# Scaling x by a product with diagonals in the prologue of a hybrid layer, and pairing the two products of a block inverse

## The reference

```python
def _rms(x, gain):
    y = xf * lax.rsqrt(jnp.mean(xf * xf, axis=-1, keepdims=True) + EPS)
    return (y * gain).astype(x.dtype)

mod = c @ p['w_ada'] + p['b_ada']
shift, scale, gate = jnp.split(mod, 3, axis=-1)
h = _rms(x, p['norm_gain']) * (1 + scale[:, None, :]) + shift[:, None, :]
... = _split_in(h @ p['w_in'])          # 9,296 columns

# in _gated_delta, per chunk of 64 tokens and head
L = jnp.where(tri_strict, jnp.einsum('bnhid,bnhjd->bnhij', kb, kc) * decay, 0.0)
tinv = lax.linalg.triangular_solve(eye + L, eye, left_side=True, lower=True)
```

## Time and profile before

| | |
|---|---|
| median of three runs | 1803.33 us (1802.0 to 1804.93) |
| the profiled execution | 1802.76 us, of which the span is 1800.9 us |
| TensorE, weight loads | 1724.2 us busy (96%), 1610.2 us (89%) |
| VectorE, ScalarE, GpSimd | 911.9 us (51%), 635.0 us (35%), 242.1 us (13%) |
| granted clock of TensorE | 0.990 of full speed on average |
| DMA queues | 286.15 MB moved, 159 GB/s over the span |

### The profile page before, as it was taken

How to read it: one execution, slowest core, us unless ns; L and a number is a source line. 1 busy time by engine, 2 the same in 40 slices (tenths; PEclk the granted TensorE clock), 3 DMA queues, 4 the chain that set the end, 5 groups by cost and what they waited for, 6 DMA issues and landing times.

```text
span 1800.9 us, 28716 instructions
## 1 busy us (share of the span) xinstructions
PE 1724.2 (96%) x11182; PEld 1610.2 (89%) x11182; DVE 911.9 (51%) x1694; ACT 635.0 (35%) x1169; POOL 242.1 (13%) x353
## 2 busy tenths in 40 slices
PE   4999999999999899999999999989999998999998
PEld 2999999999999899999999988877887897999986
DVE  4544555754564776896222244344444446563433
ACT  5523524543443532233333242334333445020200
POOL 0111111212121710421311200000000121000000
PEclk9999999999999999999999999999999998999999
DMA  9222334677876843446654230124215797652342
GB/s 339 81 84 82 105 107 149 202 238 223 271 227 193 262 158 117 145 139 203 204 179 158 96 130 24 36 84 128 60 47 199 273 356 252 210 189 72 118 140 76
DMA packets 235760, 286.15 MB, mean 159 GB/s; under 512 B 43185, under 2 KB 193230, under 8 KB 235500
## 3 DMA queue, kind: packets, MB, share of 16 engines
q1 hardware_dynamic: 227916, 280.57, 48.7%
q10 hardware_dynamic: 7552, 3.73, 0.7%
q0 software_dynamic: 160, 0.05, 0.0%
HBM read 179.39 MB, written 104.92 MB: 158 GB/s over the span
## 4 chain that ended last, share of the span: by engine, by line
PE 67%; issue 14%; DVE 5%; POOLq 4%; ACT 2%; POOL 1%; DMA 1%; DVEq 1%; SPq 1%; ACTq 0%
PE PS L2203 29%; PE PS L1056 10%; PE PS L418 7%; PE PS L1162 5%; PE PS L664 3%; PE PS L637 3%; PE PS L650 2%; POOLq L1795 1%; DVE R L2338 1%; POOLq L1793 1%; PE PS L639 1%; PE PS L638 1%; DVE hf L2350 1%; PE PS L2237 1%; POOL R L1859 1%
## 5 line engine op out<-in xcount | busy, mean ns | idle before, releaser
L2203 PE MATMUL PS<-HH,WL 128*128 128x352 f32 (+1 forms) x1728 | 385.3, 331 | 0.0
L2203 PE MATMUL PS<-HH,WH 128*128 128x352 f32 (+1 forms) x1728 | 373.3, 324 | 0.0
L2203 PE MATMUL PS<-HL,WH 128*128 128x352 f32 (+1 forms) x1728 | 372.3, 323 | 0.0
L2203 PEld LDWEIGHTS PS<-HH,WH 128*128 128x128 f32 (+1 forms) x1728 | 296.2, 188 | 0.3
L2203 PEld LDWEIGHTS PS<-HL,WH 128*128 128x128 f32 (+1 forms) x1728 | 293.5, 188 | 0.2
L2203 PEld LDWEIGHTS PS<-HH,WL 128*128 128x128 f32 (+1 forms) x1728 | 288.4, 189 | 2.9
L2325 DVE TENSOR_TENSOR WL<-Wraw,WH 128x2048 fp32r<-128x2048 f32 (+1 forms) x37 | 87.9, 2377 | 90.4 <-ACT WH L1917 89.2
L2338 DVE SCALAR_TENSOR_TENSOR R<-R,colA 128x1059 f32<-128x1059 f32 x72 | 97.2, 1349 | 5.5
L1937 ACT ACTIVATE R<-PS 128x1056 f32<-128x1056 f32 (+1 forms) x49 | 51.5, 1051 | 134.1 <-PE PS L2203 133.8
L689 ACT ACTIVATE pr<-PS,amx 128x128 f32<-128x128 f32 (+8 forms) x66 | 48.5, 734 | 127.5 <-DVE amx L730 127.5
L1056 PE MATMUL PS<-FH,VL 128*128 128x352 f32 x384 | 86.3, 333 | 4.6 <-DVE FL L980 3.4
(11 more groups left out here) (349 smaller groups left out, 2842.5 us busy)
## 6 DMA issues: line engine op xcount, KB each, us to landing
scratch_proj<-R SPq DMA_DIRECT2D x72, 576.0 KB, 3.3
Wraw<-in_w_in SPq DMA_DIRECT2D x36, 1024.0 KB, 6.9
job<-scratch_proj SPq DMA_DIRECT2D x18, 512.0 KB, 6.2
fr<-scratch_u SPq DMA_DIRECT2D x16, 528.0 KB, 5.7
gr<-scratch_proj SPq DMA_DIRECT2D x16, 528.0 KB, 3.9
job<-scratch_proj SPq DMA_DIRECT2D x9, 768.0 KB, 7.5
Wraw<-in_w_ada SPq DMA_DIRECT2D x6, 1024.0 KB, 9.5
R<-scratch_gcum SPq DMA_DIRECT2D x9, 512.0 KB, 6.3
```

Of the source, the lines that this page charges most:

```text
L2203: last = pe.matmul(PS[0:m, 3 * (p % 2) + b, 0:TB], w[:, u % 2, k, j * P:j * P + m], x[:, k, b * TB:(b + 1) * TB], start=(k == 0 and first) ...
```

## The change

In the prologue the squares of tiles 3, 8 and 7 (`X_ON_DVE`: third, fourth and eighth place of the order, counted from 0) move from ScalarE to VectorE, as one `tensor_tensor_reduce` each. VectorE no longer scales `R`; it makes a 128x128 diagonal matrix of each tile's scales in the space of `dcy`. The groups of k = 0 and 1 (`RAW` = 256 features) are made by TensorE as a full product of unscaled x with this diagonal, and the other 768 features of each tile are scaled in place by GpSimd. The first modulation columns are handled between the two sets of scales. The order of x groups, modulations and first chunk steps on TensorE is written anew, with the places where ScalarE (`n` = 6, 11, 16) and VectorE (6, 12, 18) take part in the modulation and where ScalarE splits the first weights (now n = 6).

In the side work f3 is no longer a step of its own: step f2 of tile t makes its eight products alternately with the eight f3 products of tile t - 1, and a last f2 step stands after the eighth tile. The matrices of the two lie in opposite corners: SBUF partitions 0 to 63 to PSUM partitions 64 to 127, and 64 to 127 to 0 to 63.

Semaphores that are only renamed are left out of the diff.

```diff
@@ -284,6 +284,10 @@
         return max(n for n, (kk, g) in enumerate(XG) if kk == k) + 1
 
     X_ORDER = [0, 1, 2, 3, NT, 4, 5, 6, 7]
+    X_HALVES = ((0, 5), (5, 9))
+    X_ON_DVE = (3, 4, 8)
+    RAW = 256
+    diag = dcy[:, :, :, :].rearrange("p a b c -> p (a b c)").rearrange("p (t n) -> p t n", n=P)
 
 
     def col_of(c):
@@ -1459,8 +1463,9 @@
     W_INV, N_INV = S0 // 2 + 20, 17
     F0 = 120
     for t in range(NT):
-        for i in range(3):
-            side[at(F0 + 3 * t + i)] = (f"f{i + 1}", t)
+        side[at(F0 + 3 * t)] = ("f1", t)
+        side[at(F0 + 3 * t + 1)] = ("f2", t)
+    side[at(F0 + 3 * NT - 1)] = ("f2", NT)
     L0, L_STEP, Q0, Q_STEP = 4 * 31, 6, 4 * 48, 10
     for t in range(NKT):
         if t <= NT:
@@ -1631,7 +1636,7 @@
             sp.dma_start(N21[t % 2], tile3(scr["nl"][t, 0:HB])[:, :, HB:P]).then_inc(s_fl[t % 2], 16)
 
         def inverse_out(t):
-            sp.wait_ge(s_sr, turns["f3", t] + 1)
+            sp.wait_ge(s_sr, turns["f2", t + 1] + 1)
             sp.dma_start(scr["xt"][t], XTs[t % 2].rearrange("p h n -> p (h n)")).then_inc(s_fs[t % 2], 16)
 
         def latent_in(t):
@@ -1753,10 +1758,10 @@
                     v_out(t)
                     if t + 2 <= NT:
                         v_in(t + 2)
-                if kind == "f3":
-                    inverse_out(t)
-                    if t + 2 < NT:
-                        inverse_in(t + 2)
+                if kind == "f2" and t:
+                    inverse_out(t - 1)
+                    if t + 1 < NT:
+                        inverse_in(t + 1)
                 if slot == at(S0 + 4 * NT + 6):
                     for t in range(2):
                         v_in(t)
@@ -1808,6 +1813,10 @@
         pool.dma_start(rows[72:96, 1], a["b_ada"][0].rearrange("(c p) -> c p", p=P)).then_inc(s_vecs, 16)
         for i, name in enumerate(("dn_out_norm", "q_nope_norm", "k_nope_norm")):
             pool.dma_start(rows[96 + i:97 + i, 1], a[name]).then_inc(s_vecs, 16)
+        for c, t in enumerate(X_ORDER):
+            n = rows_of(t)
+            pool.wait_ge(s_xn, c + 1)
+            pool.tensor_scalar(R[0:n, t, RAW:D], R[0:n, t, RAW:D], xst[0:n, 1, c:c + 1], None, ALU.mult).then_inc(s_pad, 1)
         pool.wait_ge(s_colc, 2)
         pool.wait_ge(s_hl, NG)
         pool.memset(stage[:, 0, TOK:TPAD], 0.0)
@@ -1900,13 +1909,14 @@
             act.activation(modr[:, i % 2], PS[0:98, 3 + i % 2, 0:P], ACT.Copy).then_inc(s_modr, 1)
         act.wait_ge(s_xst, 1)
         for n, t in enumerate(X_ORDER):
+            if n in X_ON_DVE:
+                continue
             if n == 2:
                 rows_of_modulation(0)
                 act.wait_ge(s_cols, 2)
                 act.activation(colB[:, :], PS[:, 0, 0:99], ACT.Copy).then_inc(s_colc, 1)
-            rows_t = P if t < 8 else DEC
             act.wait_ge(s_x[t // 4], 16)
-            act.activation(hf[0:rows_t, 0:2].rearrange("p a b -> p (a b)"), R[0:rows_t, t], ACT.Square, accum_out=xst[0:rows_t, 0, n:n + 1]).then_inc(s_xss, 1)
+            act.activation(hf[:, 0:2].rearrange("p a b -> p (a b)"), R[:, t], ACT.Square, accum_out=xst[:, 0, n:n + 1]).then_inc(s_xss, 1)
             act.drain()
 
         def split_hi(u):
@@ -1964,10 +1974,10 @@
         for n in range(NG):
             g, k, w = x_group(n)
             cols = slice(512 * g, 512 * g + w)
-            if n == 2:
+            if n == 6:
                 split_hi(0)
-            if n in (2, 9, 15):
-                rows_of_modulation(1 + (2, 9, 15).index(n))
+            if n in (6, 11, 16):
+                rows_of_modulation(1 + (6, 11, 16).index(n))
             act.wait_ge(s_mod, k // 2 + 1)
             act.wait_ge(s_xT, n + 1)
             if n >= NHF:
@@ -2075,10 +2085,12 @@
                 act.wait_ge(s_nas[1], 16 * (NT + 1))
             act.activation(A1, PS[0:HB, 6].rearrange("p (h n) -> p h n", h=H), ACT.Copy).then_inc(s_sr, 1)
         if kind == "f2":
-            act.activation(Pm, PS[HB:P, 7].rearrange("p (h n) -> p h n", h=H), ACT.Copy).then_inc(s_sr, 1)
-        if kind == "f3":
-            act.wait_ge(s_xi, 2)
-            act.activation(XTs[t % 2][0:HB, :, HB:P], PS[0:HB, 6].rearrange("p (h n) -> p h n", h=H), ACT.Copy).then_inc(s_sr, 1)
+            if t < NT:
+                x = act.activation(Pm, PS[HB:P, 7].rearrange("p (h n) -> p h n", h=H), ACT.Copy)
+            if t:
+                act.wait_ge(s_xi, 2)
+                x = act.activation(XTs[(t - 1) % 2][0:HB, :, HB:P], PS[0:HB, 6].rearrange("p (h n) -> p h n", h=H), ACT.Copy)
+            x.then_inc(s_sr, 1)
 
     def act_decay(act, step):
         if step == 0:
@@ -2133,12 +2145,16 @@
 
         def x_back(n):
             g, k, w = x_group(n)
-            pe.wait_ge(s_xn, (4, 9, 5)[g])
+            pe.wait_ge(s_xn if k < RAW // P else s_pad, (4, 9, 5)[g])
             if n >= 2:
                 pe.wait_ge(s_hf, n - 1 if n < 16 else max(n - 3, 15))
             for t in range(4 if g < 2 else 1):
                 r = P if g < 2 else DEC
-                last = pe.transpose(PS[:, x_bank(n), t * P:t * P + r], R[0:r, 4 * g + t, k * P:(k + 1) * P], ident[0:r, 0:r])
+                out, rows_t = PS[:, x_bank(n), t * P:t * P + r], R[0:r, 4 * g + t, k * P:(k + 1) * P]
+                if k < RAW // P:
+                    last = pe.matmul(out, rows_t, diag[0:r, X_ORDER.index(4 * g + t), 0:r], start=True, stop=True)
+                else:
+                    last = pe.transpose(out, rows_t, ident[0:r, 0:r])
             last.then_inc(s_xT, 1)
 
         def first_chunk(k):
@@ -2159,32 +2175,33 @@
         pe.transpose(PS[:, 0, 0:99], rows[0:99, 1], ident[0:99, 0:99]).then_inc(s_cols, 1)
         modulation_columns(0)
         pe.wait_ge(s_colc, 2)
-        for n in range(2):
+        for n in range(4):
             x_back(n)
         for half in range(2):
+            x_back(4 + half)
             modulation(1, half)
-        for n in range(2, 4):
-            x_back(n)
+        x_back(6)
         modulation_columns(1)
-        for n in range(4, 6):
-            x_back(n)
-        for half in range(2):
-            modulation(2, half)
-            x_back(6 + half)
+        x_back(7)
         for k in range(2):
             first_chunk(k)
             x_back(8 + k)
+        modulation(2, 0)
+        x_back(10)
+        modulation(2, 1)
         modulation_columns(2)
-        x_back(10)
+        x_back(11)
+        first_chunk(2)
+        x_back(12)
+        first_chunk(3)
+        x_back(13)
         for half in range(2):
             modulation(3, half)
-            x_back(11 + half)
-        for n in range(13, 16):
-            x_back(n)
+            x_back(14 + half)
         modulation_columns(3)
         for n in range(16, 18):
             x_back(n)
-        for k, tiles in zip(range(2, KD), ((18, 19), (20, 21), (22,), (23,), (), ())):
+        for k, tiles in zip(range(4, KD), ((18, 19), (20, 21), (22, 23), ())):
             first_chunk(k)
             for n in tiles:
                 x_back(n)
@@ -2274,10 +2291,10 @@
                 x = pe.transpose(PS[0:HB, 6, h * HB:(h + 1) * HB], XTs[t % 2][0:HB, h, 0:HB], ident[0:HB, 0:HB])
         if kind == "f2":
             for h in range(H):
-                x = pe.matmul(PS[HB:P, 7, h * HB:(h + 1) * HB], N21[t % 2][:, h], A1[:, h], start=True, stop=True)
-        if kind == "f3":
-            for h in range(H):
-                x = pe.matmul(PS[0:HB, 6, h * HB:(h + 1) * HB], Pm[:, h], XTs[t % 2][HB:P, h, HB:P], start=True, stop=True)
+                if t < NT:
+                    x = pe.matmul(PS[HB:P, 7, h * HB:(h + 1) * HB], N21[t % 2][:, h], A1[:, h], start=True, stop=True)
+                if t:
+                    x = pe.matmul(PS[0:HB, 6, h * HB:(h + 1) * HB], Pm[:, h], XTs[(t - 1) % 2][HB:P, h, HB:P], start=True, stop=True)
         x.then_inc(s_sd, 1)
 
     @block.tensor
@@ -2295,7 +2312,7 @@
     def dve_pass01(dve):
         dve.memset(PS[:, 3:5, 0:P], 0.0)
         dve.memset(xst[:, :, :], 1.0).then_inc(s_xst, 1)
-        dve.wait_ge(s_colc, 2)
+        dve.drain()
 
         def modulations(j):
             dve.wait_ge(s_modT, j + 1)
@@ -2307,17 +2324,31 @@
             dve.scalar_tensor_tensor(G[:, 2 * j:2 * j + 2], mod[:, KD + 2 * j:KD + 2 * j + 2], 1.0,
                                      colA[:, A_GAIN + 2 * j:A_GAIN + 2 * j + 2].unsqueeze(2).to_broadcast([P, 2, 2]), ALU.add, ALU.mult).then_inc(s_mod, 1)
 
-        modulations(0)
-        for lo, hi in ((0, 5), (5, 9)):
+        def squares(c):
+            t = X_ORDER[c]
+            n = rows_of(t)
+            dve.wait_ge(s_x[t // 4], 16)
+            dve.tensor_tensor_reduce(PS[0:n, 1:3].rearrange("p a b -> p (a b)"), R[0:n, t], R[0:n, t], 1.0, 0.0, ALU.mult, ALU.add, xst[0:n, 0, c:c + 1])
+            dve.drain()
+
+        def scales(lo, hi):
             ss, r, tmp = (xst[:, n, lo:hi] for n in range(3))
-            dve.wait_ge(s_xss, hi)
```

(25 more changed lines are left out.)

## The result

| | before | after |
|---|---|---|
| median (20 runs each, side by side) | 1803.37 us (1801.39 to 1807.37) | 1808.02 us (1803.6 to 1816.05) |
| profiled execution, its span | 1802.76, 1800.9 us | 1807.21, 1805.3 us |
| first chunk step, chunk 1 | 41.14, 63.66 us | 46.23, 76.59 us |

The ratio is 1.003, with a 95% interval of 1.0022 to 1.0038: the change costs 4.0 to 6.9 us. The prediction said 1802.5, and most likely no change.

The account below looks back on a forecast made before the run. TensorE, 96% busy, was taken to pace the first pass from chunk 1 on. Prologue +4.7, inverse -7.4 and stall +2.0 gave -0.7 us on 1802.76, stated as 1802.5, range 1797.3 to 1809.0.

Parts of the forecast that it names:

- no change: Whole kernel: gain and loss cancel, 1802.5 us against the profiled 1802.76; chance 0.42.
- The start: Prologue: TensorE's first x product at 23.5 us instead of 28.07, 4.6 us earlier.
- GpSimd's scaling: Prologue: nine in-place scalings of 768 columns at 1.2 us each, costing nothing up to 1.75.
- GpSimd late: Prologue rival: above 1.75 us a scaling holds group 7; at 2.4, +6 us, 1808.5; chance 0.10.
- Early products: Prologue, TensorE: a large x group made as an fp32 diagonal product takes 0.9 us; four add 2 us.
- the slower bound: Prologue: first chunk step at 41.5 us with early products at the slower rate; as a rival, 1806.4 and more, chance 0.08.
- The new order: Prologue, first chunk step to chunk 1: 22.4 us of work plus four waits, 6.5 in sum, makes 28.9 us.
- The inverse: Inverse products at 868 to 1046 us: paired corners overlap, 1.35 us a double step, 7.4 us saved.
- The stall: Inverse, a tile's transpose waiting on a late store and reload: 2.0 us added, bounds 0 and 4.
- the bound of 4: Inverse: upper bound in us of the 2.0 added for waiting at a tile's transpose.
- The sum: Chunk 1 starts at 68.3 us, 4.7 lost; with 7.4 saved and 2.0 added in the inverse, -0.7 overall.
- is carried to the end of the span: First pass: TensorE paces it from 63.66 us, so any gain or loss before chunk 1 stays to the end.

Follow-up runs that it names:

- the two-input run: The changed kernel with GpSimd's nine scalings as a product of two tensors, the scale broadcast over 768 columns: 1810.34 us, 1.0034 of before.
- the 512-column kernel with GpSimd: The changed kernel with 512 instead of 256 columns of x taken through diagonals, GpSimd scaling the other 512: 1811.9 us, 1.0042 of before.
- the kernels with VectorE's scalings: The changed kernel with VectorE, not GpSimd, scaling the 768 columns: in the new order 1803.71 us, 1.0003 of before; in the old order 1795.64 us, 0.9959.
- the kernel with the shared squares: The kernel before with paired inverse products, three tiles' squares on VectorE and modulation 0 behind the first five scalings, no diagonals: 1800.39 us, 0.9978.
- The kernel with the prologue alone: The changed kernel with the inverse products put back as before, three steps a tile: 1815.37 us, 1.0058 of before.
- the run without that term: The changed kernel with VectorE, not GpSimd, scaling columns 256 to 1023 after its nine diagonals: 1803.71 us, 1.0003 of before.

## Why the prediction was wrong, step by step

- **The start: right.** First x product forecast at 23.5, measured 23.89. The eleven small steps took the 2.65 us of the rows; the five diagonals took 1.6 us for 0.85, one of them 0.84 beside GpSimd, and ScalarE's sums were 0.4 earlier than taken.
- **GpSimd's scaling: the step that failed.** The prediction took 1.2 us, "one input being nearer to the cast", and named 1.75 as the threshold and 2.41 as the far bound. Measured: 2.28 at the median, 2.52 as a mean (22.71 over nine), close to the far bound, the mean above it. So its rival "GpSimd late", given 0.10, came, with its place (group 7), its end (forecast 45, measured 45.4) and nearly its price: 6 forecast, about 5 by two of three pairs of kernels. The choice between two rows that differ in form was made by the number of inputs, and that was the wrong likeness: the two-input product in the same place took 1.47. The Trainium skill ("GPSIMD Engine Reference", Elementwise — side-by-side cycle accounting) gives GpSimd about 2.6 cycles an element at 1.2 GHz for a `tensor_tensor`, measured there on an add, and about 1.8 at best. For 768 columns that is an estimate of 1.66 and 1.15 us; the two-input run, at 1.47, lies between, below the page's rate for its own form, and the scaling by one value a partition, at 2.28, lies above both.
- **Early products: mis-sized.** 0.9 taken for a large diagonal group, 2.0 measured between 24 and 35 us, at the lower clock. At the upper one, at 49.26 us in the 512-column kernel with GpSimd, the same group took 1.16. The prediction set the column's 1.00 against the slow rows of before, kept both rates and took 39.4, nearer the quicker one's 38.4 than the slower one's 41.5. In every trace TensorE's work up to 31 us is at the slower rate, so the slower bound was the one to take; without GpSimd it came at 42.29, for 39.4 taken. Those 2.9 us are this term and the hand-overs behind it; no run separates them.
- **The new order: right in its waits, too small in its worth.** Forecast 0.4, 2.0, 1.8 and 2.3; measured 0.40, 1.75, 1.20 and 2.08. From first chunk step to chunk 1 28.9 was forecast; it was 30.4, of which 1.4 is the first step at half clock. The waits were 1.1 us less than forecast, so that the sum came near is in part luck. The order's total is about 8 us by whole runs and 7.1 at the start of chunk 1 between the kernels with VectorE's scalings (72.45 and 65.31). There it is a first chunk step 0.8 later (42.29 for 41.45), since modulation 1 behind six x groups holds the low split; 3.6 of waits behind it (5.4, where the old order has 1.85); and 2.1 for the two halves of modulation 2, which the old order makes in front of the first chunk step. The other 0.6 is not accounted for. Each of the two kernels has one stretch at the lower clock, here behind the 2.32 us wait, there behind the waits of 1.24 and 0.45 us in front of chunk step 2.
- **The inverse: right in its mechanism.** 1.35 was taken for a double step with its edges; measured are 1.07 to the next main matmul and 0.1 in that one's longer row, so 1.2. The stall was 1.49 for 2.0, at the tile named. In the trace 7.3 us are won over the inverse (9.45 behind to 2.15), for 5.4 forecast. By whole runs of the paired products alone it is 3 to 5 us. There the stall was 1.81 and 3.88 in the traces, and a stretch at the lower clock followed both, which the forecast had no term for; the stall of 4.30, in the kernel with the shared squares, lies above the bound of 4. Behind the inverse the changed kernel falls back by 2.2 us, in part at a lower clock (0.71 from 1055 to 1060). The kernel with the prologue alone, which has no pairing, falls back there too, from 13.7 to 15.7, so part of this may lie in the one profiled execution of before.
- **The sum.** At chunk 1: 4.7 forecast, 12.9 measured, = 4.7 + 6.8 (first chunk step 46.23 for 39.4) + 1.5 (30.4 for 28.9), to rounding. Of the 6.8, 3.9 is GpSimd (46.23 - 42.29) and 2.9 the early products and hand-overs. The 7.3 of the inverse would leave 5.6; the medians are 4.7 apart, and 4.4 in the profiled executions, since 3.5 are made up in front of the inverse and 2.2 lost behind it. That the kernel without GpSimd's scalings comes out at no change, as forecast, is partly luck: there the early products cost 2.9 more and the inverse won 1.9 more than taken. The prediction's premise that what is lost before chunk 1 "is carried to the end of the span" held only in part here.

Left open: why doubling the diagonal share makes loads late far behind the prologue; and how the lag of 12.9 us shrinks to 9.45 before the first inverse step. The profiles differ there in stretches of lower granted clock, as at 380 to 400 us, where before has 0.91 and after 1.00, but no experiment isolates them.

## What to carry to other kernels

Ask what ends the last wait in front of the step that matters before making its input earlier: here x came 3.6 to 4.2 us sooner and the step that wanted it did not move, because a load and another engine's queue ended there. When an operation goes to an engine on which the trace has no row of the same form, find the price from which it decides, and if that price lies inside your bounds treat it as undecided; choosing by likeness cost this forecast its sign, as the run without that term shows (1.0003 for 1.0030). Price early TensorE work at the slower rate that its own early rows show, whatever the clock column reads there. The kernel with the lowest ratio keeps the old order and VectorE's scalings, with the paired products: 0.9959, where the paired products alone gave 0.9971 and 0.9983, so most of its gain is the pairing and the rest can't be told from nothing.

## What the runs showed of the hardware

- GpSimd multiplies 128x768 fp32 by one value a partition in 2.28 us and by a broadcast second input in 1.47 (medians); VectorE does the first in 0.60.
- The quicker form is dear for the neighbour: VectorE's 128x128 product rises from 0.28 to 1.45 us beside it. Beside the slower form single ones rise too (0.17 to 0.65 for an instruction on 128x4, 0.28 to 0.85 for a diagonal), but the median stays at 0.28. The Trainium skill ("GPSIMD Engine Reference", Specifications), which the prediction quoted, has the two engines share their SBUF interfaces; the traces agree. Most of the loss is VectorE's, but GpSimd loses too: its scaling beside VectorE's two-input low split took 4.08 us (4.30 in the old order), for 2.28.
- Products of 64x64 at opposite corners, with different weights of 64 columns, overlap entirely: 16 in the 1.07 us of 8 (at 906.82).
- The same TensorE work took nearly twice as long before 35 us as after it (a half modulation 1.89 at 33.33 and 1.06 at 36.85). That is the 1.2 GHz level: six traces read 0.50 there over the same rows, and the 1.00 of the other eight stands in front of their first record of the clock. After the 5.35 us wait it reads 0.50 again, for 45 to 50.
